# A gate projection whose squares, root and gated sums stand elsewhere, and another order of the second mixers' steps

## Chip, cores and metric

One core of a Trainium2 chip runs the whole program once. The metric is the device time of one execution in microseconds (us), the median of several; lower is better.

## What is computed

Two transformer blocks over 256 tokens of width 1024, in float32 accuracy. The change touches the seam between them: the gated addition that ends the first block, the two norms behind it, and the mixers of the second block.

```python
# end of the first block
g = jax.nn.sigmoid(rmsnorm(h, norm_ple_g) @ ple_gate)
h = h + g * (p @ ple_proj)
x = rmsnorm(h, final_norm_g)
# second block
proj = rmsnorm(x, mix_norm_g) @ w_in          # (256, 2328)
conv_a, conv_b, q, k_c, v_c, k_s, v_s, k_w, v_w, gate_logits = jnp.split(proj, IN_SPLITS, axis=-1)
y_conv = silu(layernorm(depthwise_conv31(conv_a * sigmoid(conv_b)), ...))
y_nsa = nsa_mixer(q, k_c, v_c, k_s, v_s, k_w, v_w, gate_logits, ...)   # three attentions, rotary on q, k_s, k_w
h = x + jnp.concatenate([y_conv, y_nsa], axis=-1) @ w_out
h = h + memory_attention(...)
h = h + peer(...)
```

## The kernel before, in words

Every dense product streams its weights from HBM in units of 128 x 1024 floats (four units a chunk, four buffers `raw`). ScalarE (ACT) rounds a unit's two halves into `w_hi` (`split_hi`, L421), VectorE (DVE) or GpSimd (POOL) subtracts the rest into `w_lo` (`split_lo`, L428), and TensorE (PE) makes three products with `x_hi` and `x_lo` (L494). There are two slots of `w_hi` and `w_lo`, so a unit's split can begin only when PE has used the unit two before it. `s_use1`, `s_use` count units used (first, second half), `s_hi1`, `s_hi`, `s_lo1`, `s_lo` the split halves, `s_ev` the chunks evacuated. All queues are in order: a wait holds back all that stands behind it on its engine.

**The gate projection** (`ple_and_norm`) has two chunks, one for each half of the 1024 columns. `split_chunks` emits, for ACT and for DVE, a body for the first chunk (not "hooked": units 2 and 3, then unit 0 of the next chunk, with the `lead` functions behind unit 2, 3 and `UNITS`), and a "hooked" body for the second (unit 1, hook 0, units 2 and 3, hook 1, unit 0 of what follows). On ACT the first body has the squares of `h` behind units 2 and 3 (`own_square`, L1870) and the square root behind unit 0 of the next chunk (`own_root`, L1875); DVE inverts it (`own_inverse`, L1879). In the second body, ACT's hook 0 waits for all products of the first chunk and makes the first half's gates, one sigmoid for each token tile (L1891); hook 1 squares `h` and `xn` (L1916). DVE's hook 0 (`gated_sum`) waits for `s_ev`, then makes for each of the two token tiles a product with `ple` (L1903), the sum into `h` (L1905) and the gained copy `xn` (L1907), all ahead of the split of unit 2. PE's last unit does token tile 0, then the transposes of the new `h` (L893), then tile 1.

Behind the two bodies stand the second half's gates (L1932), the `x_hi` and `x_lo` of the next projection (L902, L909), sums (L1937, L1939) and, last on DVE, the second half's gained copies (L1953, tokens `gained`).

**The second mixers** (`mixers_2`) are six strands of steps, each a Python generator: `d` dense (12 units of w_in in token-major form, 4 steps each, then 8 units in feature-major form, then w_out's 8 units), `c` conv taps on PE and the layer norm, `t` conv taps on DVE (11 taps of 4 tiles, L2126 and L2130), `k` keys and token tile 0 of the attention, `q` queries and token tile 1, `n` the norm. `weave` takes them in the order of the letters of `MIXERS_2_ORDER` and puts each step's instructions at the ends of the engines' queues; a step whose inputs aren't emitted yet gives nothing. When the letters are used up, the strands go on in turn. The dense strand's step that begins unit 1 has `other_half`: PE transposes the other half of `h` and ACT and DVE make its `x_hi` and `x_lo`. The steps of `n` are: squares of `h` and `xn` for tile 0 (L2000, L2002), the same for tile 1, a bias from them on DVE (L2006 to L2009), the roots (L2013), the inverse (L2016), then the inverse turned by PE (L2022). The first chunk's evacuation (L704) waits for the inverse. `c` begins with an identity and the diagonals of the first taps on POOL (L2082, L2078). The half of a unit that POOL splits is the first.

## Time and profile before

| | |
|---|---|
| median of 3 runs | 1627.99 us (1622.12 to 1630.15) |
| the profiled execution | 1626.81 us, its span 1624.8 us |
| mean granted clock of TensorE | 0.985 |
| PE | 1553.3 us busy (96%) |
| DVE | 1183.0 us (73%) |
| ACT | 858.5 us (53%) |
| POOL | 342.6 us (21%) |
| end of the gate projection's first chunk | about 497 us |
| second mixers, w_in | 511.8 to 594.1 us |
| second mixers, no dense products | 594.1 to 676 us |
| w_out | from 676 us |

PE is busy nearly all the time over the whole span, so the thing to read is where it is not, and where its granted clock is low: in those places something else sets the pace. A line of the timeline ends with the idle time of its engine before it and the instruction that ended it. In a table of stretches, each engine's busy time is followed by its number of instructions; PEclk is the granted clock as a share of 2.4 GHz.

### The profile page before, as it was taken

Reading aid. Unit: us, or ns where it says so; the run is one execution under the profiler, and the core shown is the slowest. Engines: PE = TensorE matmul, PEld = TensorE weight load, DVE = VectorE, ACT = ScalarE, POOL = GpSimd, SP = SyncE. Lnnn points to the kernel's source line nnn. Section 1 sums busy time; section 2 is a strip of 40 time slices with the busy share of each in tenths; the row PEclk is TensorE's granted clock in tenths of the full one; section 3 lists DMA queues with packets and bytes.
Section 4 is the critical chain, followed back from the end, with each engine's and each line's share of the span. In section 5 each row is a group of like instructions: output and inputs, shape, how many; then the busy total and the mean of one; then the engine's idle time right before and its main releaser. Section 6 shows DMA issues by size and latency. Waiting matters only on the chain.

```text
span 1624.8 us, 31457 instructions
## 1 busy us (share of the span) xinstructions
PE 1553.3 (96%) x10528; PEld 1409.2 (87%) x10528; DVE 1183.0 (73%) x2258; ACT 858.5 (53%) x1573; POOL 342.6 (21%) x257
## 2 busy tenths in 40 slices
PE   8899998999998888999999999999999999999997
PEld 8789987999876776898998999988888999999996
DVE  3788676788657558555489677779998777776776
ACT  5664445656557644566455455554444454445444
POOL 3334322011000501132057755530000000000000
PEclk9999999999999988999999999999999999999999
DMA  7333244555565610164546644467777665566554
GB/s 278 118 112 97 92 143 163 169 169 179 183 194 155 241 42 1 53 202 148 167 146 206 201 146 137 142 191 242 241 243 224 197 190 182 192 182 190 184 186 149
DMA packets 87847, 271.14 MB, mean 167 GB/s; under 512 B 9824, under 2 KB 26336, under 8 KB 87392
## 3 DMA queue, kind: packets, MB, share of 16 engines
q1 hardware_dynamic: 65088, 237.01, 45.8%
q10 hardware_dynamic: 22688, 33.17, 6.5%
q8 instruction: 47, 0.77, 0.2%
q14 instruction: 24, 0.20, 0.0%
HBM read 258.60 MB, written 11.53 MB: 166 GB/s over the span
## 4 chain that ended last, share of the span: by engine, by line
PE 81%; DVE 9%; ACT 4%; issue 3%; POOL 2%; DMA 1%; ACTq 1%; DVEq 0%; SPq 0%; POOLq 0%
PE ps_chunk L494 44%; PE ps_misc L494 21%; PE ps_misc L295 7%; PE ps_misc L2729 4%; PE ps_chunk L295 2%; ACT w_hi L421 1%; DVE ffn_arena L1743 1%; POOL w_lo L428 1%; DVE w_lo L428 1%; PE ps_misc L936 1%; PE ps_chunk L501 1%; DMA raw<-in_stream 0%; ACT ffn_arena L1727 0%; PE ps_chunk L936 0%; POOL mixers_arena L2078 0%
## 5 line engine op out<-in xcount | busy, mean ns | idle before, releaser
L421 ACT ACTIVATE w_hi<-raw 128x512 fp32r<-128x512 f32 (+1 forms) x900 | 548.7, 626 | 490.2 <-PE ps_chunk L494 284.4
L428 DVE TENSOR_TENSOR w_lo<-raw,w_hi 128x512 fp32r<-128x512 f32 x671 | 488.1, 743 | 270.7 <-ACT w_hi L421 260.8
L494 PE MATMUL ps_chunk<-x_hi,w_hi 128*128 128x256 f32 x1792 | 518.7, 289 | 14.4 <-POOL w_lo L428 7.3
L494 PE MATMUL ps_chunk<-x_hi,w_lo 128*128 128x256 f32 x1792 | 508.2, 284 | 0.0
L494 PE MATMUL ps_chunk<-x_lo,w_hi 128*128 128x256 f32 x1792 | 507.9, 283 | 0.0
L428 POOL TENSOR_TENSOR w_lo<-raw,w_hi 128x512 fp32r<-128x512 f32 (+2 forms) x229 | 298.9, 1319 | 542.8 <-ACT w_hi L421 479.6
L494 PEld LDWEIGHTS ps_chunk<-x_hi,w_hi 128*128 128x128 f32 x1792 | 344.3, 192 | 27.3 <-POOL w_lo L428 12.7
L494 PEld LDWEIGHTS ps_chunk<-x_hi,w_lo 128*128 128x128 f32 x1792 | 344.8, 192 | 2.8 <-issue 0.2
L494 PEld LDWEIGHTS ps_chunk<-x_lo,w_hi 128*128 128x128 f32 x1792 | 344.5, 192 | 0.0
L494 PE MATMUL ps_misc<-w_hi,hid_hi 128*128 128x512 f32 x520 | 203.5, 391 | 2.1 <-DVE hid_lo L2808 1.4
L494 PE MATMUL ps_misc<-w_hi,hid_lo 128*128 128x512 f32 x520 | 203.1, 391 | 0.0
L494 PE MATMUL ps_misc<-w_lo,hid_hi 128*128 128x512 f32 x520 | 202.3, 389 | 0.0
L295 PE MATMUL ps_misc<-mixers_arena 128*128 128x128 f32 (+7 forms) x840 | 116.3, 298 | 7.7 <-ACT mixers_arena L1393 2.8
L295 PEld LDWEIGHTS ps_misc<-mixers_arena 128*128 128x128 f32 (+1 forms) x840 | 105.6, 198 | 15.7 <-ACT mixers_arena L966 3.4
L494 PEld LDWEIGHTS ps_misc<-w_hi,hid_hi 128*128 128x128 f32 x520 | 97.9, 188 | 21.7 <-issue 1.6
L494 PEld LDWEIGHTS ps_misc<-w_lo,hid_hi 128*128 128x128 f32 x520 | 97.6, 188 | 20.9
L494 PEld LDWEIGHTS ps_misc<-w_hi,hid_lo 128*128 128x128 f32 x520 | 97.9, 188 | 17.6
L494 PE MATMUL ps_chunk<-w_hi,x_hi 128*128 128x512 f32 (+2 forms) x256 | 102.2, 399 | 5.6 <-DVE w_lo L428 3.2
L494 PE MATMUL ps_chunk<-w_hi,x_lo 128*128 128x512 f32 (+2 forms) x256 | 98.0, 383 | 0.0
L494 PE MATMUL ps_chunk<-w_lo,x_hi 128*128 128x512 f32 (+2 forms) x256 | 97.7, 382 | 0.0
L2804 DVE TENSOR_TENSOR xn<-row,peer_arena 128x256 f32<-128x256 f32 x128 | 80.7, 631 | 10.1 <-PE ps_misc L494 7.4
L2719 DVE TENSOR_TENSOR xn<-ident_iota,ps_chunk 128x512 f32<-128x512 f32 x64 | 43.8, 684 | 43.1 <-PE ps_misc L2729 39.5
(372 smaller groups left out, 1724.1 us busy)
## 6 DMA issues: line engine op xcount, KB each, us to landing
raw<-in_stream SPq DMA_DIRECT2D x452, 512.0 KB, 3.6
early_rows<-row ACTq DMA_DIRECT2D x64, 128.0 KB, 1.7
row<-early_rows ACTq DMA_DIRECT2D x62, 128.0 KB, 3.3
memory_kv<-mixers_arena ACTq DMA_DIRECT2D x4, 512.0 KB, 4.9
mixers_arena<-in_cmp_w ACTq DMA_DIRECT2D x1, 2048.0 KB, 10.3
mixers_arena<-memory_kv ACTq DMA_DIRECT2D x4, 512.0 KB, 6.8
mixers_arena<-in_consts ACTq DMA_DIRECT2D x1, 1729.0 KB, 9.0
row<-in_rows ACTq DMA_DIRECT2D x3, 512.0 KB, 7.3
```

Source lines behind the costliest of these rows:

```text
L295: return lambda e: e.matmul(out, lhsT, rhs, start=start, stop=stop, skip_group_check=True)
L421: e.activation(w_hi[q % 2][:, s], raw[q][:, s], ACT.Copy).then_inc(made, 1)
L428: e.tensor_tensor(w_lo[q % 2][:, s], raw[q][:, s], w_hi[q % 2][:, s].bitcast(F32), ALU.subtract).then_inc(made, 1)
L494: last = e.matmul(o, stationary[a], moving[b], start=start and i == 0, stop=stop and i == 2, skip_group_check=True)
L501: e.matmul(o, a[:, k * P:(k + 1) * P], x_hi[:, k, :], start=start and i == 0, stop=False, skip_group_check=True)
L936: done = pe.do(lambda e, i=i, s=s: e.transpose(ps[0:rows_out, i * P:(i + 1) * P], s, ident), *needs, *free)
L1743: e.scalar_tensor_tensor(out=o, in0=ps_chunk[slot][:, piece * T:(piece + 1) * T - lag], scalar=col[:, bass.ds(at + (2 - lag), 1)], in1=o, ...
L2719: e.tensor_tensor(cols_hot[g % 2], same, against(1), ALU.is_equal).then_inc(s_eq, 1)
L2729: last = e.matmul(ps_misc[:, g, i * P:(i + 1) * P], cols_hot[g % 2][:, i, :], rows_hot[g % 2][:, i, :], start=True, stop=True)
L2804: e.tensor_tensor(own[b], gel[slot], g, ALU.mult).then_inc(s_own, 1)
```

## The change

In the gate projection: ACT's first square goes ahead of unit 2, the second behind unit 2, the root behind unit 3, and a one-column sigmoid stands where the root stood, so the sigmoid's table is loaded there. DVE's inverse goes behind unit 3. `gated_sum` is split by token tile: tile 0 behind unit 1 and tile 1 behind unit 2 of the second chunk, each waiting for its own gate; the gained copies go behind unit 3, and the squares of the gained copies move to two new steps of `n` in the second mixers. The strings of the order differ throughout: 358 letters for 352, `n` 8 for 6, `d` 134 for 130, the others alike.

```diff
-MIXERS_2_ORDER = ("dddddddnndddnnndnkqddddqdddcdddddddddddqdddddddddddkqddddddckdkddddddddkcqdddddddddtdcqkkddqdtdddkdqdkcddkk"
-                  "kkkkkkcqddqdcdkqktddkdqqqkcddtqttttctktctkqttttdkcttttccttttddktttcqqkkkqqtdtttdqdtdkcttddktddctcqdd"
-                  "cctctdcdcttcckdqqtkktdkttdqqtdttcqddtttttttdcckkdttdttqqtckttqtccttdtdcdccdcccccdccddkddckddddkqktqq"
-                  "ccdcdtdtdqcccccccdkcddkqqdckkdqqkcqkqccckqqkc")
+MIXERS_2_ORDER = ("ndncddddnddddcnkddtnddddndnnqcdddddqdddddddtdddddkddddddddddqddkdkcdddqddddqddddkdddddddkkqkdddkqdkd"
+                  "qqdcdddkkkkdctkqkddddkddkktcqqqdddkkddcqqtdkdtktttttttdcttdkddtqddttddttktkktddccqqqttkcqddddddqkttt"
+                  "ttttcdcctdttcttktddkdqqkctttqcccccdttqtctttdkdttttttkkctttdtqtctkqqcdcddtckttcctqqttcccccccdcktcddcc"
+                  "kqkqqtcdcccckkdddddccccqqctkddcqccddkkkqccdddqkqkqdcqdkqcd")
...
                     def after(u):
-                        if not hooked and u in lead:
-                            lead[u](e)
+                        at = ("next", u) if hooked else u
+                        if at in lead:
+                            lead[at](e)
                     for q in range(begin, 2):
                         split(e, q, n)
                     hook(0)
+                    after(0)
                     for q in range(2, UNITS):
...
-            def gated_sum(e, slot, m):
-
-                if m != first:
-                    return
-                cols = halves[0]
-                e.wait_ge(s_ev, first + 1)
-                for t in range(TT):
+            def gated_sum(t):
+
+                def run(e):
+                    cols = halves[0]
+                    e.wait_ge(s_gate_0, t + 1)
                     e.tensor_tensor(gate[:, t, cols], gate[:, t, cols], ple[:, t, cols], ALU.mult).then_inc(s_ple, 1)
                     e.wait_ge(s_ple, t + 1)
                     e.tensor_tensor(h[:, t, cols], h[:, t, cols], gate[:, t, cols], ALU.add).then_inc(s_ple_sum[t], 1)
-                    e.wait_ge(s_ple_sum[t], 1)
-                    e.tensor_tensor(xn[:, t, cols], h[:, t, cols], row[:, cols], ALU.mult).then_inc(s_gain[t], 1)
...
+            def first_gains(e, slot, m):
 
                 if m == first:
                     cols = halves[0]
-                    for src, made, at, over in ((h, s_ple_sum, PART, gate), (xn, s_gain, 10, ple)):
-                        for t in range(TT):
-                            e.wait_ge(made[t], 1)
-                            e.activation(over[:, t, cols], src[:, t, cols], ACT.Square,
-                                         accum_out=ss[:, at + t:at + t + 1]).then_inc(s_square, 1)
+                    for t in range(TT):
+                        e.wait_ge(s_ple_sum[t], 1)
+                        e.tensor_tensor(xn[:, t, cols], h[:, t, cols], row[:, cols], ALU.mult).then_inc(s_gain, 1)
+
+            def first_squares(e, slot, m):
+
+                if m == first:
+                    cols = halves[0]
+                    for t in range(TT):
+                        e.wait_ge(s_ple_sum[t], 1)
+                        e.activation(gate[:, t, cols], h[:, t, cols], ACT.Square,
+                                     accum_out=ss[:, PART + t:PART + t + 1]).then_inc(s_square, 1)
+
+            def sigmoids_table(e):
+                e.activation(ss[:, 24:25], c("one"), ACT.Sigmoid)
...
-            split_chunks(first, count, act_hooks=(hook, first_squares), dve_hooks=(gated_sum,), ahead=1,
-                         act_lead={2: own_square(0), 3: own_square(1), UNITS: own_root}, dve_lead={UNITS: own_inverse})
+            act.quiet(own_square(0))
+            split_chunks(first, count, act_hooks=(hook, first_squares), dve_hooks=(None, first_gains), ahead=1,
+                         act_lead={2: own_square(1), 3: own_root, UNITS: sigmoids_table},
+                         dve_lead={3: own_inverse, ("next", 0): gated_sum(0), ("next", 2): gated_sum(1)})
...
-                    both = act.do(lambda e, t=t: e.activation(scratch, xn[:, t, half], ACT.Square,
-                                                              accum_out=ss[:, 2 + t:3 + t]), gained[t])
+                    act.do(lambda e, t=t: e.activation(scratch, xn[:, t, half], ACT.Square,
+                                                       accum_out=ss[:, 2 + t:3 + t]), gained[t])
                     yield
-                dve.wait((s_square, 2 * TT))
+                for t in range(TT):
+                    both = act.do(lambda e, t=t: e.activation(scratch, xn[:, t, 0:CW], ACT.Square,
+                                                              accum_out=ss[:, 10 + t:11 + t]), first_gained)
+                    yield
+                dve.wait((s_square, TT))
```

## Rows read from the trace of the kernel before

**Rows 1.** Stretches: length, busy us of each engine, granted clock, DMA share, GB/s

```profile
511.80:551.30 39.50, 33.07 (x163) 26.77 (x163) 24.81 (x52) 25.52 (x53) 14.89 (x13) 0.96 0.68 236
...
551.30:594.10 42.80, 38.97 (x289) 37.82 (x288) 17.93 (x31) 21.49 (x35) 13.41 (x10) 0.88 0.34 109
...
594.10:676.00 81.90, 70.44 (x642) 54.77 (x639) 66.50 (x139) 37.93 (x103) 6.48 (x3) 0.87 0.01 1
```

**Rows 2.** Timeline, gate projection; start, us, engine, line, operation, [idle before <-releaser]

```profile
500.52 0.69 DVE L1903 TENSOR_TENSOR ffn_arena<-ffn_arena 128x512 f32<-128x512 f32 x1 [1.92 <-ACTq L1894]
...
505.37 0.50 PE L494 MATMUL ps_chunk<-w_hi,x_hi 128*128 128x512 f32 x1 [2.74 <-DVE w_lo L428]
...
511.39 0.39 PE L494 MATMUL ps_chunk<-w_hi,x_lo 128*128 128x512 f32 x1
...
511.61 0.39 PE L494 MATMUL ps_chunk<-w_lo,x_hi 128*128 128x512 f32 x1
```

**Rows 3.** Timeline of ACT, the first half's gates

```profile
497.88 1.28 ACT L1891 ACT_TABLE_LOAD   x1
...
499.18 1.26 ACT L1891 ACTIVATE ffn_arena<-ps_chunk,ss 128x512 f32<-128x512 f32 x2
```

**Rows 4.** Timeline, start of the second mixers, ACT, DVE, POOL and PE

```profile
515.73 1.57 ACT L902 ACTIVATE x_hi<-ps_misc,ss 128x256 fp32r<-128x256 f32 x4 [1.59 <-PE ps_misc L878]
...
516.17 1.28 DVE L1953 TENSOR_TENSOR xn<-h,row 128x512 f32<-128x512 f32 x2
...
517.17 1.17 ACT L421 ACTIVATE w_hi<-raw 128x512 fp32r<-128x512 f32 x2
...
517.96 1.28 POOL L428 TENSOR_TENSOR w_lo<-raw,w_hi 128x512 fp32r<-128x512 f32 x1 [91.62 <-ACT w_hi L421]
...
518.21 0.64 ACT L2000 ACTIVATE picks<-h 128x512 f32<-128x512 f32 x1
...
519.30 0.50 PE L494 MATMUL ps_chunk<-w_hi,x_hi 128*128 128x512 f32 x1 [0.65 <-POOL w_lo L428]
...
521.14 0.19 ACT L2002 ACTIVATION_READ_ACCUMULATOR picks<-xn 128x1 f32 x1
...
525.39 0.48 PE L2022 MATMUL ps_misc<-ident_iota,picks 128*128 128x128 f32 x1 [3.75 <-DVE picks L2019]
```

**Rows 5.** Timeline of POOL and PE, the diagonals of the conv taps

```profile
548.55 0.32 POOL L2082 TENSOR_TENSOR mixers_arena<-ident_iota 128x64 f32<-128x64 f32 x1
...
548.95 5.17 POOL L2078 TENSOR_TENSOR mixers_arena<-mixers_arena,col 128x1280 f32<-128x1280 f32 x2
...
555.43 0.38 PE L494 MATMUL ps_chunk<-x_hi,w_hi 128*128 128x256 f32 x1 [1.08 <-POOL w_lo L428]
```

**Rows 6.** Timeline of DVE and POOL, a pair that overlaps later

```profile
631.41 2.67 POOL L2078 TENSOR_TENSOR mixers_arena<-mixers_arena,col 128x1280 f32<-128x1280 f32 x1 [13.99 <-PE ps_chunk L295]
...
631.97 2.13 DVE L1010 TENSOR_TENSOR mixers_arena<-mixers_arena 128x4 f32<-128x4 f32 x1
```

**Rows 7.** Timeline of PE and DVE, rotary embedding and last dense product

```profile
567.01 0.41 PE L936 MATMUL ps_misc<-ident_iota,mixers_arena 128*64 128x128 f32 x2 [1.52 <-DVE mixers_arena L2226]
...
592.01 0.30 PE L936 MATMUL ps_misc<-ident_iota,mixers_arena 128*64 128x128 f32 x1 [1.23 <-DVE mixers_arena L2226]
...
592.56 0.63 PE L295 MATMUL ps_misc<-mixers_arena 128*64 128x30 f32 x6
...
594.14 0.69 DVE L708 TENSOR_TENSOR mixers_arena<-ps_chunk,picks 128x512 f32<-128x512 f32 x1 [1.87 <-PE ps_chunk L494]
```

**Rows 8.** Busy times by stretch, two stretches at a low clock

```profile
524.90:528.40 3.50, 3.01 (x8) 2.48 (x9) 2.40 (x7) 0.87 (x2) 0.79 (x1) 0.51 1.06 296
...
579.60:589.80 10.20, 10.20 (x51) 10.09 (x51) 1.49 (x2) 3.81 (x7) 1.28 (x1) 0.50 0.15 51
```

**Rows 9.** DVE in the stretch without dense products: busy times, then who waited

```profile
594.00:665.50 71.50, 60.04 (x547) 44.37 (x545) 62.86 (x133) 33.26 (x93) 5.04 (x2) 0.86 0.01 1
...
DVE mixers_arena L979 <- PE ps_misc L295: 5.1, 7, 2.5
```

More of the change, by code:

```diff
@@ L1905, in gated_sum @@
                     e.tensor_tensor(h[:, t, cols], h[:, t, cols], gate[:, t, cols], ALU.add).then_inc(s_ple_sum[t], 1)
-                    e.wait_ge(s_ple_sum[t], 1)
-                    e.tensor_tensor(xn[:, t, cols], h[:, t, cols], row[:, cols], ALU.mult).then_inc(s_gain[t], 1)
+                return run
+            def first_gains(e, slot, m):
[4 more added lines that the diff above has]
+                        e.tensor_tensor(xn[:, t, cols], h[:, t, cols], row[:, cols], ALU.mult).then_inc(s_gain, 1)
             def first_squares(e, slot, m):
@@ L1912, in first_squares @@
                     cols = halves[0]
-                    for src, made, at, over in ((h, s_ple_sum, PART, gate), (xn, s_gain, 10, ple)):
-                        for t in range(TT):
-                            e.wait_ge(made[t], 1)
-                            e.activation(over[:, t, cols], src[:, t, cols], ACT.Square,
-                                         accum_out=ss[:, at + t:at + t + 1]).then_inc(s_square, 1)
+                    for t in range(TT):
[4 more added lines that the diff above has]
+                e.activation(ss[:, 24:25], c("one"), ACT.Sigmoid)
             s_gate_0 = sem("s_gate_0")
             s_ple, s_square = sem("s_ple"), sem("s_square")
-            s_gain = [sem(f"s_gain{t}") for t in range(TT)]
+            s_gain = sem("s_gain")
             dve.wait(have_gain)
             act.wait(*added[1])
-            split_chunks(first, count, act_hooks=(hook, first_squares), dve_hooks=(gated_sum,), ahead=1,
-                         act_lead={2: own_square(0), 3: own_square(1), UNITS: own_root}, dve_lead={UNITS: own_inverse})
+            act.quiet(own_square(0))
+            split_chunks(first, count, act_hooks=(hook, first_squares), dve_hooks=(None, first_gains), ahead=1,
+                         act_lead={2: own_square(1), 3: own_root, UNITS: sigmoids_table},
+                         dve_lead={3: own_inverse, ("next", 0): gated_sum(0), ("next", 2): gated_sum(1)})
             second = first + 1
@@ L1954, in ple_and_norm @@
                              sum_made[t], own=False) for t in range(TT)]
-            return next_x, both_gains, sum_made, gained, s_square
+            return next_x, both_gains, sum_made, gained, s_square, (s_gain, TT)
         def own_norm(*turned):
@@ L1966, in own_norm @@
             return act.do(lambda e: e.activation(h[:, 1, :], xn[:, 1, :], ACT.Copy, scale=ss[:, 17:18]), inverse)
-        next_x, both_gains, sum_made, gained, s_square = ple_and_norm(added)
+        next_x, both_gains, sum_made, gained, s_square, first_gained = ple_and_norm(added)
         def mixers_2():
@@ L2001, in norm @@
                            sum_made[t])
-                    both = act.do(lambda e, t=t: e.activation(scratch, xn[:, t, half], ACT.Square,
-                                                              accum_out=ss[:, 2 + t:3 + t]), gained[t])
+                    act.do(lambda e, t=t: e.activation(scratch, xn[:, t, half], ACT.Square,
+                                                       accum_out=ss[:, 2 + t:3 + t]), gained[t])
                     yield
-                dve.wait((s_square, 2 * TT))
+                for t in range(TT):
[3 more added lines that the diff above has]
+                dve.wait((s_square, TT))
                 dve.do(lambda e: e.tensor_scalar(bias, ss[:, PART:PART + TT], EPS / D, EPS * EPS, ALU.mult, ALU.add))
                 dve.do(lambda e: e.scalar_tensor_tensor(out=bias, in0=ss[:, 10:12], scalar=1.0 / D, in1=bias,
-                                                        op0=ALU.mult, op1=ALU.add))
+                                                        op0=ALU.mult, op1=ALU.add), both)
                 v = dve.do(lambda e: e.scalar_tensor_tensor(out=bias, in0=ss[:, 16:18], scalar=EPS / D, in1=bias,
-                                                            op0=ALU.mult, op1=ALU.add), both)
+                                                            op0=ALU.mult, op1=ALU.add))
                 yield
```

## Prediction

> **What bounds the kernel now.** I read the page's busy times first (PE 96% of the span), then the busy times of five stretches around the change, then the waits of PE in each, and last the timeline of each engine at those waits. PE sets the pace, so only its idle time and its stretches at a low clock can be won. From the first unit of w_in to the last product before w_out they are large [rows 1]: 6.4 us of 39.5 idle, then 3.8 of 42.8, then 11.5 of 81.9, with mean granted clocks of 0.96, 0.88 and 0.87 of 2.4 GHz. In the first two PE waits for single late instructions. In the third DVE is the fuller engine: 62.9 of 71.5 us busy, where 5.1 us of its idle time waits for PE's scores [rows 9]. So there the length is that of DVE's queue, and an order can win only DVE's few gaps. Earlier, in the gate projection, PE stands still for 2.74 us until DVE has split unit 2 [rows 2].
>
> **The change part by part.** The sum is made on the profiled execution, 1626.8 us, which is 1.2 below the median of 1628.0.
>
> *1. Gate projection: -2.7 us.* DVE makes six operations of 0.69 us from 500.52, then the split, and PE goes on at 505.37 [rows 2]. After the change only two of the six stand ahead of the split. They also start sooner: the sigmoid's table (1.28 us, at 497.88) is loaded before the products end, and DVE waits for one gate, not for both (1.26 us the pair) [rows 3]. I put the start near 499, the two operations until 500.4, ACT's rounding of unit 2, which stands behind the gates, at 499.6 to 500.3, and so the split's first half at about 501.1. PE asks for it at 502.6. The cover is 1.5 us; unit 3 has two more operations ahead of its split, and some 1.3 us of cover. Squares and root come 1.2 to 2.5 us sooner on ACT, ahead of unit 2's rounding; PE has two units (12 products of 0.22 to 0.23 us each, 2.7 us [rows 2]) before it asks for that one. Moved squares cost ACT as much as before. Next late in this place: nothing within 0.5 us. The whole stall goes.
>
> *2. Start of the second mixers: +0.7 us, between -1.5 and +4.2.* I work in the clock of the old trace; all of it slides by part 1. The new order begins `n`, `d`, `n`: four squares now stand on ACT ahead of the step that holds `other_half`. Two of them wait for the gained copies, which are DVE's last work, 516.17 plus 1.28 us [rows 4]. So ACT, in order, is held: the first gained square can start at 516.9, and three more follow at 0.8 (four took from 518.21 to 521.33), until 519.3. Only then come the other half's `x_hi` (1.57, which had begun at 515.73), the rounding of unit 2 (0.6 for its first half) and POOL's part (1.28): PE can begin unit 2 at 522.8, not at 519.30. PE ended unit 1 at 518.65, so its idle time here grows from 0.65 to 4.15 us. Against that, the turned inverse now stands behind 16 dense steps instead of 11, and PE's 3.75 us idle before L2022 [rows 4] has five steps (3.4 us) to hide behind. But the `c` step with the diagonals is now emitted inside unit 2, so 0.32 + 5.17 us of POOL [rows 5] lie between its parts of units 3 and 4: unit 3's ends at about 524.8, the diagonals at 530.3, unit 4's (0.8, it is narrow) at 531.1. PE, two units and the turn later, would be there at 528.9. In the old trace it reached unit 4 at about 530.5, so we lose some 0.6. Behind it the first chunk's evacuation and the rounding of unit 5 keep this distance; own_norm now stands behind unit 6's rounding, a small gain I leave out. The low clock after the old wait, 3.5 us at 0.51 [rows 8], has a counterpart after the new one, which the wait for POOL covers. Bounds: -1.5 if POOL's diagonals stop nobody, +4.2 if the new idle time comes on top of the old.
>
> DVE's small operations meet the diagonals as well. Once, in the old trace, a 128x4 product with two inputs beside POOL's 2.67 us multiplication took 2.13 us and ended with it [rows 6]. Here the bias, unit 4's second half and the wide copy of the inverse would wait in that manner, until 530.6, and the turn until 531.6; with that, unit 4 starts at 531.9 and not at 531.1, and I use 0.7 as the middle. The Trainium skill (SBUF — State Buffer, Who interferes with whom) has this as a rule that speaks against the change: a VectorE instruction with two SBUF inputs and a GpSimd one that reads SBUF exclude each other for their whole length. Without the rule the loss would be 0.6, by it 1.4; the pair of rows agrees with it.
>
> *3. Diagonals gone from their old place: -1.1 us.* There they stood ahead of POOL's part of a split, and PE waited 1.08 [rows 5]. Between 0 and -1.1.
>
> *4. Rotary embedding of the keys: -1.5 us.* PE waited 1.52 for it [rows 7]; its DVE step was emitted behind the evacuation of unit 15's chunk and unit 16's first product. The new order emits it ahead of both, directly behind unit 15's last step, while PE still has most of that unit (2.9 us) to do. Between 0 and -1.5.
>
> *5. End of the dense products: -2.4 us.* The queries' rotation stood ahead of the last dense steps and held PE for 1.23; six dense steps now lie between the rotation and its first turn, where two did. Four turns (0.55 to the next start) and six small products (0.56) stood ahead of the last dense step and now stand behind it [rows 7]. DVE is idle for 1.87 at that moment, waiting for that last product, so DVE's queue starts sooner by all of it. Between -0.5 and -2.4.
>
> *6. Clock: 0, between 0 and -3.8 us.* PE is at half clock for 10.2 us from 579.6 [rows 8], 3.2 us into a run of 56 small products of 30 columns (the compression's). The new order cuts this run to 32, then lays dense steps between. If the clock stays up, 17 dense products of 0.21 us shrink to 0.12 and 30 small ones of 0.20 to 0.12: 1.6 + 2.2. No row says at which length it falls, and 32 still last about 3.9 us, so I take 0.
>
> *7. The stretch without dense products: 0, between -4 and +5.* It has the same 43 taps, softmaxes and norm on DVE (one of the 44 taps lies earlier in both orders). It begins sooner by what parts 1 to 5 bring, and since DVE's queue sets its length it ends sooner by as much. Bounds: DVE's waits for PE of 5.1 us [rows 9] nearly gone, or doubled.
>
> Sum: -2.7 + 0.7 - 1.1 - 1.5 - 2.4 = -7.0, 1619.8 us on the profiled execution, 1621.0 on the median's scale. I say 1620.5, a little for the open side of part 6. After w_out nothing is changed and PE is full, so nothing is given back there.
>
> **The rivals.** *More than that:* the clock stays up in the compression (-3.8) and DVE's gaps in the last stretch shrink by half (-2.5): 1614. For it: the order is wholly new in that stretch, and its 0.86 mean clock [rows 9] leaves room. Against: DVE's work there is fixed. *The gains are absorbed:* parts 3 to 5 shift waits only, because the last stretch's DVE queue waits for PE elsewhere, or part 2 comes out at +4; the gate's 2.7 remains: 1625.5. To it belongs that the gate's stall doesn't go, because another wait (a split's ACT half) takes its place. *Slower:* in the last stretch the new order puts score products and the DVE step that reads them side by side at six of the eight large softmaxes, where the old did so at three, and the last exponentials of both tiles follow one another with little of DVE's work between. Where DVE isn't behind PE at such a place, it waits for the products, as once for 2.47 us (half of the 5.1 in rows 9). Six such waits and one exponential (2 us) are some 17 us, 12 more than now: 1633. It decides as soon as DVE's idle time in this stretch grows by more than 7 us.
>
> **How the numbers follow.** Forecast (1616 to 1625): 0.45. More: 0.23. Absorbed: 0.20. Slower: 0.12. The unknown costs reach from about -15 to +9 in all; to leave out no more than two in ten I take 1612 to 1631. Half a per cent is 8.1 us, about what a measurement of this kernel can tell from none (its three runs lie 8 apart). Below 1619.9 lie the second case and some 0.17 of the first: 0.40. Above 1636.1 lies part of the last and what I have not seen: 0.08. The rest, 0.52, is within it.
>
> **What would show it.** Right: no wait of PE between the first chunk's end and the turn in the gate projection; one wait of about 4 us before unit 2 of the second mixers; the wait before L2022 gone or under 1 us; the diagonals at about 520 to 528; no wait of PE for L2226; the last dense product 6 to 9 us sooner; DVE over 85% busy from there to the layer norm. Wrong: a wait for a split in the gate projection; a second long wait at unit 4; DVE under 80% busy in the last stretch, or waiting for PE over 10 us; the low clock again at length while dense products run.

## The result, and the profile after

The changed kernel takes 1632.99 us in the median (1626.08 to 1639.35, 14 runs), the kernel before beside it 1627.12 (1621.84 to 1630.15, 14 runs): ratio 1.0040 [1.0024, 1.0056]. The medians lie 5.9 us apart, where 7 us less were forecast, and the time is outside the range. Both profiled executions begin the gate projection within 0.05 us of each other (485.75 and 485.80), so their times can be set side by side.

| | before | after | difference |
|---|---|---|---|
| profiled execution (span) | 1626.81 (1624.8) | 1637.04 (1634.9) | +10.2 |
| mean granted clock | 0.985 | 0.975 | |
| first product of the second mixers | 511.8 | 508.8 | -3.0 |
| last dense product of w_in | 593.8 | 589.0 | -4.8 |
| first value product of the attention | 660.38 | 655.56 | -4.8 |
| first product of w_out | 675.96 | 684.33 | +8.4 |

The changed kernel is ahead until the value products begin and behind when they end. Of the 1.8 us that come on top behind w_out's first product, 1.0 are its first products, which still run at half clock. The stretches, as [rows 1, 8, 9] had them (length, busy us of PE, PE's weight loads, DVE, ACT, POOL with their counts, then the granted clock, the DMA share and GB/s):

```profile
506.60:546.40 39.80, 34.12 (x172) 27.88 (x171) 26.06 (x43) 27.65 (x59) 13.85 (x13) 0.96 0.67 236
546.40:589.20 42.80, 39.96 (x284) 39.35 (x282) 24.66 (x44) 20.99 (x34) 14.35 (x10) 0.84 0.35 108
589.20:684.60 95.40, 82.79 (x652) 67.49 (x652) 66.45 (x138) 38.18 (x106) 6.19 (x3) 0.76 0.03 10
...
588.90:660.40 71.50, 58.89 (x542) 43.46 (x540) 62.31 (x132) 33.72 (x96) 4.74 (x2) 0.85 0.02 7
```

The third stretch is 13.5 us longer than in [rows 1], PE is 12.4 us busier in it, and its clock is 0.76 instead of 0.87; DVE does the same work (66.45 and 66.50 us). So the time didn't go into a wait: PE does the same products more slowly. PE's timeline of the changed kernel shows which:

```profile
647.18 0.66 PE L938 MATMUL ps_chunk<-ident_iota,mixers_arena 128*128 128x128 f32 x4
...
651.03 1.11 PE L938 MATMUL ps_misc<-ident_iota,mixers_arena 128*128 128x128 f32 x4 [3.19 <-DVE mixers_arena L1013]
651.93 1.06 PE L938 MATMUL ps_chunk<-ident_iota,mixers_arena 128*128 128x128 f32 x4
653.80 1.97 PE L938 MATMUL ps_misc<-ident_iota,mixers_arena 128*128 128x128 f32 x8 [0.81 <-DVE mixers_arena L1013]
...
655.56 13.75 PE L295 MATMUL ps_misc<-mixers_arena 128*128 128x64 f32 x64
669.11 1.92 PE L938 MATMUL ps_chunk<-ident_iota,xn 128*128 128x128 f32 x8
670.81 13.75 PE L295 MATMUL ps_misc<-mixers_arena 128*128 128x64 f32 x64
```

and that of before the same place, which the prediction didn't look at:

```profile
655.74 1.97 PE L936 MATMUL ps_chunk<-ident_iota,mixers_arena 128*128 128x128 f32 x8 [3.68 <-DVE mixers_arena L2112]
657.50 3.08 PE L936 MATMUL ps_misc<-ident_iota,mixers_arena 128*128 128x128 f32 x12
...
660.38 7.80 PE L295 MATMUL ps_misc<-mixers_arena 128*128 128x64 f32 x64
668.01 1.04 PE L936 MATMUL ps_chunk<-ident_iota,xn 128*128 128x128 f32 x8
668.89 7.26 PE L295 MATMUL ps_misc<-mixers_arena 128*128 128x64 f32 x64
```

These are the 128 value products (probabilities by values, 64 columns each). With the eight transposes between they last 15.8 us in before and 29.0 in after: 13.2 us, all at one place. The busy times over just that stretch, after:

```profile
655.60:684.60 29.00, 29.00 (x138) 29.00 (x138) 8.47 (x11) 8.13 (x14) 1.45 (x1) 0.50 0.07 19
```

and before:

```profile
660.40:676.20 15.80, 15.80 (x138) 15.80 (x138) 8.43 (x12) 8.13 (x14) 1.44 (x1) 0.96 0.00 1
```

PE is busy without a gap in both; the granted clock is 0.50 (1.2 GHz) in one and 0.96 in the other. In the records the low clock lasts from 654.7 to 661.5 us in before and from 649.0 to 686.6 in after. It falls in a wait in both, the 3.68 and the 3.19 us one. In before it is back 1.1 us into the value products and stays; in after it doesn't come back while they run, only 2.2 us after w_out's wide products have begun. The Trainium skill (TensorE: Matmul & The Clock Gate, HAM oscillation) tells of such falls in waits, and these two rows agree. They also show the clock staying low while PE is busy for 29.00 of 29.00 us.

### The profile page after: what moved, and what is told of

It is laid out like the page before. It is cut to its first block, busy times and chain, and to the rows that moved or that the text cites. A ratio compares the mean times of both kernels' runs of the same rounds, so it can differ in the third digit from the quotient of the medians.

```text
span 1634.9 us, 31462 instructions
## 1 busy us (share of the span) xinstructions
PE 1566.6 (96%) x10528; PEld 1424.1 (87%) x10528; DVE 1189.1 (73%) x2258; ACT 857.5 (52%) x1574; POOL 342.3 (21%) x257
## 4 chain that ended last, share of the span: by engine, by line
PE 80%; DVE 9%; ACT 4%; issue 3%; DMA 1%; POOL 1%; ACTq 1%; DVEq 0%; SPq 0%; POOLq 0%
PE ps_chunk L496 43%; PE ps_misc L496 21%; PE ps_misc L295 8%; PE ps_misc L2744 3%; PE ps_chunk L295 2%; POOL w_lo L428 1%; ACT w_hi L421 1%; DVE ffn_arena L1745 1%; DVE w_lo L428 1%; DMA raw<-in_stream 1%; PE ps_misc L938 1%; PE ps_chunk L503 1%; DVE mixers_arena L2145 0%; ACT ffn_arena L1729 0%; PE ps_chunk L938 0%
## 5 line engine op out<-in xcount | busy, mean ns | idle before, releaser
L496 PEld LDWEIGHTS ps_chunk<-x_hi,w_hi 128*128 128x128 f32 x1792 | 345.5, 193 | 29.9 <-POOL w_lo L428 12.4
L295 PE MATMUL ps_misc<-mixers_arena 128*128 128x128 f32 (+7 forms) x840 | 128.4, 319 | 7.7 <-ACT mixers_arena L968 3.2
L295 PEld LDWEIGHTS ps_misc<-mixers_arena 128*128 128x128 f32 (+1 forms) x840 | 117.5, 217 | 15.6 <-issue 3.8
## 6 DMA issues: line engine op xcount, KB each, us to landing
mixers_arena<-in_cmp_w ACTq DMA_DIRECT2D x1, 2048.0 KB, 10.2
```

What stands on the lines that cost most here:

```text
L295: return lambda e: e.matmul(out, lhsT, rhs, start=start, stop=stop, skip_group_check=True)
L496: last = e.matmul(o, stationary[a], moving[b], start=start and i == 0, stop=stop and i == 2, skip_group_check=True)
```

## Experiments

Each profile, of one execution, gives the length of the 128 value products, with the transposes between them. Each ratio, with its 95% interval in brackets, is to executions of the kernel before that ran beside that experiment, so it isn't the median over one fixed number.

| kernel | median (range, runs) | ratio to before | value products |
|---|---|---|---|
| changed kernel | 1632.99 (1626.08 to 1639.35, 14) | 1.0040 [1.0024, 1.0056] | 29.0 us |
| gate_only | 1622.49 (1618.47 to 1626.31, 10) | 0.9962 [0.9934, 0.9990] | 15.7 |
| order_only | 1635.51 (1631.02 to 1642.76, 10) | 1.0045 [1.0009, 1.0080] | 22.9 |
| warm_av | 1629.72 (1622.23 to 1637.68, 10) | 1.0014 [0.9992, 1.0036] | 15.2 |
| warm_gap | 1626.68 (1617.97 to 1630.60, 10) | 1.0005 [0.9983, 1.0028] | 15.2 |
| tail_old | 1621.79 (1618.71 to 1625.37, 10) | 0.9952 [0.9922, 0.9981] | 15.2 |
| diag_late | 1634.99 (1629.45 to 1638.97, 10) | 1.0039 [1.0014, 1.0065] | 23.0 |
| squares_late | 1629.87 (1623.99 to 1637.82, 10) | 1.0016 [0.9994, 1.0038] | 29.0 |
| warm_before | 1629.85 (1625.53 to 1633.88, 10) | 1.0009 [0.9993, 1.0026] | 15.2 |
| one_letter | 1626.46 (1620.12 to 1628.35, 10) | 0.9987 [0.9957, 1.0016] | 15.2 |
| tail_new | 1636.57 (1632.43 to 1641.85, 10) | 1.0055 [1.0023, 1.0086] | 29.0 |
| three_moves | 1619.17 (1616.66 to 1623.18, 12) | 0.9959 [0.9938, 0.9980] | 15.2 |
| fill_gap | 1624.62 (1619.38 to 1629.16, 10) | 0.9983 [0.9967, 0.9999] | 15.2 |

### Which half of the change costs

`gate_only` has the changed gate projection with the old order, in which two more `n` stand behind the first two, for the two new steps. `order_only` has the old gate projection with the new order.

```diff
-MIXERS_2_ORDER = ("dddddddnndddnnndnkqddddqdddcddddd"
+MIXERS_2_ORDER = ("dddddddnnnnddddnnndnkqddddqdddcddddd"
...
```

> The gate projection's change alone: the old order, with only two letters n put behind the first two for the two squares that moved (1.6 us of ScalarE). Theory one (the order brought TensorE's half clock onto the attention's value products, and that is the loss): 2.7 us won in the gate projection, up to 1.6 given back ahead of the turned inverse, the value products at the clock of the kernel before (16 us for 128 rows), so 0.997 to 1.000 of the time before. Theory two (the gate's change itself costs, by its squares in the second mixers): 1.003 or more, with the last dense product of w_in no sooner than 593.8 us.

> The new order alone, on the gate projection of before. Theory one: as in the changed kernel the value products fall into a stretch at 1.2 GHz (29 us instead of 16), and the gate's 2.7 us are missing, so 1.004 to 1.007. Theory two (the gate's change costs): 0.996 to 1.000.

The gate projection alone makes the kernel faster, 0.9962; the order alone makes it slower, 1.0045, as much as the whole change. `gate_only` reaches its first unit of the second mixers 3.1 us sooner. It then pays back 2.1 of them (1.5 by a longer wait: 5.28 us idle ahead of the turned inverse, where before had 3.75 [rows 4], since two more squares stand in front of the roots), and has them again at the last dense product (3.8 us sooner). `order_only` is 5.2 us ahead of before at the last dense product and 5.6 behind at w_out; its clock is low for 20.5 us, over the first 64 value products and the beginning of the others (13.75 us for 64, then 7.65).

### Products to keep PE at work

`warm_av` adds 16 products whose results nobody reads ahead of the value products; `warm_gap` adds 12 in PE's idle time behind the first transposes of the layer norm, and 8 ahead of the value products. `warm_before` is the kernel before with those 20.

```diff
+                if t == 0:
+                    pe.wait(*free)
+                    for _ in range(16):      # 8 in warm_gap and warm_before
+                        pe.quiet(mm(ps, x_hi[:, 0, 0:P], x_hi[:, 0:2, :].rearrange("p k t -> p (k t)")))
                 for hd in range(NSA_H):
```

> The changed kernel with 16 further products of 512 columns in front of the attention's value products, into the bank that these then overwrite (their results are used by nobody). Theory one: 16 products cost 3.7 us at full and 7 us at half clock; they bring the clock to 2.4 GHz, the 128 rows of value products take 16 us instead of 29, so 6 to 9 us less than the changed kernel: 0.998 to 1.000 of before. Rival (the clock is not what costs, or busy products here do not raise it): 4 to 7 us more than the changed kernel, 1.006 or more.

> The changed kernel with 12 such products in TensorE's idle gap of 3.2 us before the last softmaxes and 8 in front of the value products. Theory one: the 12 cost nothing (2.8 us in a gap of 3.2) and keep the clock from falling, the 8 cost 1.9 us at full clock, so 9 to 12 us less than the changed kernel: 0.996 to 0.999 of before, and no stretch at half clock from 649 to 686 us. Rival: 2 to 5 us more than the changed kernel.

> The kernel before, with 20 added products of 128 columns by 256, whose results nobody reads: 12 in PE's idle time behind the first turn of the layer norm, 8 ahead of the value products (the same two places in which they brought the changed kernel 6 us). Theory (clock): before already runs its value products at full clock in most of its executions, so the added products bring 0 to 2 us: median 1625 to 1627, ratio 0.998 to 1.001. Rival (the products help anything): they bring as much here as in the changed kernel, 4 to 6 us, and then their gain there says nothing of what the new order lost. Rival (they cost): each product of 0.11 us lies on the path, 20 of them 2 us: 1628 to 1629.

With added work PE keeps or regains the clock, and the changed kernel gets 4 to 6 us back (by the ratios) although it has more to do. Both come out some 2 us dearer than expected (1.0014 and 1.0005, where at most 1.000 and 0.999 were), which their intervals don't exclude as noise. In `warm_gap` the 12 products (3.02 us) fill most of the wait, and no low clock is recorded there at all. In the kernel before the same 20 products bring nothing (1.0009), so what they heal is something that the changed kernel has and the kernel before, in most of its executions, has not. (An added product is 128x512 in the rows, about 0.25 us at full clock and 0.5 at half; the expectation of `warm_before` took it to be 0.11.)

### The last letters of the order

`tail_old` is the changed kernel with the last 54 letters of the old order. The lines are the ends of the two orders. `tail_new` is the kernel before with the last 57 letters of the new order. In both one `t` (a tap on DVE) ahead of these letters is left out or put in, so that their number stays 67.

```diff
-kqkqqtcdcccckkdddddccccqqctkddcqccddkkkqccdddqkqkqdcqdkqcd
+kdddkqktqqccdcdtdtdqcccccccdkcddkqqdckkdqqkcqkqccckqqkc
```

> The changed kernel, with the last 54 letters of its order (from the seventh mask softmax to the layer norm's second step) taken from the order of before; everything up to some 640 us stands as in the changed kernel. Theory (clock): what PE does in the last 10 us ahead of the value products sets the clock in which they run. In before it is 3.7 us of idle time in one piece, then transposes and products close together, and PE is at full clock again within 1 us of the first value product; in the changed kernel it is 3.2 us, then a few products, then 0.8 us more, and the 128 products take 29.0 us instead of 15.8. With the old tail the profile should show the value products at full clock (16 to 18 us), w_out's first product 8 to 12 us sooner than in the changed kernel, and a median of 1621 to 1627. Rival (queue): the new order's loss comes from DVE's and ACT's order in the whole stretch from 590 us on, and the clock only follows; then the last letters alone bring less than 2 us and the value products still take over 25 us. Rival (phase): the outcome depends on the instant at which the stretch falls, not on its order; then the run to run spread stays as wide as the changed kernel's (1626 to 1639) with the median between the two.

> The kernel before (its gate projection, its order), with only the last 57 letters of its order taken from the changed kernel's. Theory (clock): this is the new order's whole loss, carried into the old kernel: the value products run at half clock (25 to 29 us instead of 15.8) in most executions, w_out's first product comes 9 to 13 us later, median 1634 to 1640, ratio 1.005 to 1.008. Rival (queue): the loss is spread over the stretch from 590 us on, then under 3 us come with these letters (1626 to 1630). Rival (phase): the instant matters and not the order; the old kernel comes to this place some 5 us later than the changed one, and the clock then may stay full: 1626 to 1630 with a wide spread.

It works in both directions. The old tail takes the changed kernel from 1.0040 to 0.9952; the new tail takes the kernel before from 1 to 1.0055. No engine's work differs, only its order. The stretch of the value products in `tail_new`:

```profile
658.50:687.50 29.00, 29.00 (x138) 29.00 (x138) 8.49 (x11) 8.13 (x14) 1.45 (x1) 0.50 0.07 19
```

and in `tail_old`:

```profile
654.10:669.40 15.30, 15.30 (x139) 15.30 (x138) 8.81 (x12) 8.49 (x15) 1.44 (x1) 1.00 0.00 1
```

In `tail_new` the clock had fallen before the long wait (2.73 us here), at 645.9 us, in a run of 16 products behind a wait of 1.72:

```profile
645.24 4.93 PE L295 MATMUL ps_misc<-mixers_arena 64*128 64x128 f32 x16
```

The same 16 last 3.00 us in before.

Is it the instant that decides, and not the order? Not alone: `tail_new` and `tail_old` come to their value products at 658.5 and 654.1 us (655.6 in after, 660.4 in before), and each has the clock that its last letters give it. The mean clocks of all executions say the same: with the new tail (after, `order_only`, `diag_late`, `squares_late`, `tail_new`) it is 0.978 or less in 29 of 54, with the old tail or one of the two repairs below (`gate_only`, `tail_old`, `three_moves`, `one_letter`, `fill_gap`) in none of 52. But the instant has a part. In after and `squares_late` the clock falls 2 us before the long wait ends and stays low for 37.5 us; in `order_only` and `diag_late`, with the same last letters, it falls within 0.4 us behind the wait's end and stays low for 20.5. And the kernel before pays at times too: in 9 of 103 executions it took 1638.6 to 1643.9 us at a mean clock of 0.973 to 0.977, in all others 1633.2 or less. That the value products were slow in those nine is likely by the size of the step, but none of them was profiled. So the order sets how often this is paid, not whether in each execution.

### What in the last letters

In the new tail four transposes of the layer norm (tile 0) stand ahead of PE's long wait, which leaves it 3.19 us long, and a wait of 0.81 lies behind it, between two groups of eight. In the old tail all of the layer norm's transposes are behind the long wait, and PE has 20 products without a gap before the value products. `one_letter` moves one `c`, those four transposes, ten letters back:

```diff
-kqkqqtcdcccckkdddddccccqqctkddcqccddkkkqccdddqkqkqdcqdkqcd
+kqkqqtcdcccckkdddddccccqqctkddcqccddkkkqcdddqkqkqdccqdkqcd
```

> The changed kernel, with one letter of its order moved: the layer norm's turn of tile 0 (four products of PE) ten letters later, directly ahead of that of tile 1. In the changed kernel PE does these four before a 3.19 us wait, then runs 8 products, waits 0.80 us, runs 8 more and begins the value products, all at half clock to 686.6 us. With the letter moved the long wait begins some 0.65 us sooner (3.8 us, as in before), and 12 products or more follow it close together. No work, no wait of DVE and no length of anything else is changed. Theory (clock): if how PE's work lies in these few us sets the clock of the value products, this letter alone may bring it back: value products 16 to 18 us instead of 29.0, w_out's first product 8 to 12 us sooner, median 1622 to 1628. Rival (more is needed): the 0.80 us wait that stays, or the smaller amount of work, is enough to leave the clock low; then nothing changes (1631 to 1635), and the cause lies in the rest of the last letters.

One letter takes the ratio from 1.0040 to 0.9987. Its timeline of PE has the 20 products in one piece, and the value products at full clock:

```profile
656.15 1.12 PE L938 MATMUL ps_misc<-ident_iota,mixers_arena 128*128 128x128 f32 x4 [3.78 <-DVE mixers_arena L1013]
657.06 1.92 PE L938 MATMUL ps_chunk<-ident_iota,mixers_arena 128*128 128x128 f32 x8
658.93 1.57 PE L938 MATMUL ps_misc<-ident_iota,mixers_arena 128*128 128x128 f32 x8
...
660.33 7.26 PE L295 MATMUL ps_misc<-mixers_arena 128*128 128x64 f32 x64
```

But the letter changes two things, the length of the long wait and the gap behind it. `fill_gap` leaves the long wait and puts four unread products into the gap:

```diff
                                  copy_evac(act, PT[:, (t + 1) * b + k, g * 512:(g + 1) * 512]))
+                        if (t, b, g) == (0, 1, 1):
+                            busy_pe(4)
```

> The changed kernel with 4 added products of 128 columns by 256, whose results nobody reads, directly behind the transposes of tile 0's last softmax: they fall into the 0.80 us in which PE waits for tile 1's last multiplication, and last some 0.9 us at half clock. The 3.19 us wait ahead of them stays as it is. Theory (the short gap): PE must be at work without a break behind the long wait for its clock to rise before the value products begin; then these 4 products alone bring it back in most executions: value products 15 to 18 us instead of 29.0, median 1622 to 1628. Rival (place of the long wait): it is where and how long PE waits ahead of this (3.19 us here, 3.7 to 3.8 in the kernels that kept the clock) that counts; then the value products stay at 25 to 29 us and the median at 1631 to 1635.

```profile
655.41 0.89 PE L946 MATMUL ps_misc<-ident_iota,mixers_arena 128*128 128x128 f32 x4 [3.19 <-DVE mixers_arena L1021]
655.95 2.06 PE L295 MATMUL ps_misc<-x_hi 128*128 128x512 f32 x4
657.81 1.05 PE L946 MATMUL ps_chunk<-ident_iota,mixers_arena 128*128 128x128 f32 x4
658.65 1.26 PE L946 MATMUL ps_misc<-ident_iota,mixers_arena 128*128 128x128 f32 x8
659.75 2.46 PE L295 MATMUL ps_misc<-mixers_arena 128*128 128x64 f32 x21
```

The wait of 3.19 us is still there, the gap of 0.81 is not, and the clock is back at 659.1 us, 0.6 ahead of the value products, which take 15.2 us. So what PE does between the long wait and the value products is enough to decide it, with the long wait as it was. The profiled execution alone wouldn't show it, since its clock fell only at 655.7 us, just behind the wait's end, and not 2 us before it as in after; but none of the ten executions is over 1629.16 us or under a clock of 0.981, where 11 of the changed kernel's 14 take longer than 1631. The four products (2.06 us) do more than fill 0.81 us, though: whether it is the gap's absence or their added work that counts, these runs don't tell apart.

### The two early waits of the new order

`squares_late` puts the first two steps of `n` back behind seven dense steps; `diag_late` issues POOL's diagonals 37 letters later. The lines are the starts of the orders of the changed kernel and `squares_late`.

```diff
-ndncddddnddddcnkddtn
+dddddddnncnddcnkddtn
```

> The changed kernel, with the first 16 letters of its order rearranged (the same letters): the two square steps of the norm stand behind the first seven dense steps, as in before, not ahead of the first. Theory (held ACT): PE's 3.99 us of idle time ahead of unit 2 is ACT's queue, held by the squares that wait for DVE's gained copies; it falls to 0.6 to 1 us, and unit 2 comes 3.0 to 3.4 us sooner. Whether that stays: if it does, the last dense product is 3 us sooner too (median 1629 to 1631 with the clock over the value products as in the changed kernel). Rival (inverse): the turned inverse then is the next late thing, since its squares end no sooner, and PE waits 2 to 4 us ahead of its product (L2022) or for the first chunk's evacuation; the last dense product is then less than 1 us sooner and the early wait of the new order costs nothing by itself.

> The changed kernel, with one conv step of its order moved: the first of the two that stand ahead of the diagonals goes 37 letters later, so that POOL's 0.32 and 4.89 us multiplications are issued behind unit 18 rather than beside the keys' and queries' rotation angles. Theory (port): in the changed kernel DVE's small two-input operations beside these multiplications take 2.2 us each instead of 0.17, the split behind them is late, and PE waits 2.84 us for it. Without the neighbour these operations take under 0.5 us, this wait of PE goes (0 to 0.5 us), and the last dense product comes 2.5 to 3 us sooner than in the changed kernel; the median, with the clock over the value products unchanged, 1629 to 1632. Rival (queue): the split is late because of the amount of work that the rotation angles put ahead of it on DVE, whoever stands beside it; then the wait shrinks by less than 1.5 us. Rival (moved): the diagonals now stand ahead of POOL's part of a split near unit 18 and PE waits there for as long as it did before (1.1 us or more).

In `squares_late` unit 2 is at once 3.4 us sooner (0.65 us idle instead of 3.99), but waits of 1.74 and 2.05 us for POOL's part of a split follow at units 3 and 5, and by the end of the token-major units 0.6 are left. That is the size that the rival forecast, though not its wait: PE stands only 0.36 us ahead of the turned inverse. Behind it the wait at the diagonals is longer than the changed kernel's 2.84 us, and the last dense product is 2.0 us later than there:

```profile
552.24 0.58 PE L496 MATMUL ps_chunk<-x_hi,w_hi 128*128 128x256 f32 x1 [4.26 <-DVE w_lo L428]
```

In `diag_late` the 2.84 us stall is gone, no idle time over 0.5 us is left between 539 and 592 us, and no wait takes its place; a small DVE operation that took 2.23 us takes 0.17:

```profile
548.35 0.17 DVE L2254 TENSOR_SCALAR mixers_arena<-mixers_arena 128x16 f32<-128x16 f32 x1
```

Yet the last dense product is only 0.55 us sooner than in after, where 2.5 to 3 were expected. In this execution, as in that of `tail_old`, whose first 66 letters are the same, ACT had to wait for the weights of unit 8, by 2.6 and 2.2 us. The row of `tail_old`:

```profile
535.49 1.15 ACT L421 ACTIVATE w_hi<-raw 128x512 fp32r<-128x512 f32 x2 [2.19 <-DMA raw<-in_stream]
```

That wait is 1.3 us in after and 1.6 in two pieces in before. What sets its length isn't shown. It isn't being ahead of time alone: `gate_only`, 1 to 2 us ahead of before there, has no such wait, `three_moves`, some 4 ahead, one of 0.6 us, and `order_only`, behind it, one of 1.8. `diag_late`'s median (1634.99) is no better than the changed kernel's, and it keeps the new tail, and the low clock with it.

### All three moves

> The changed kernel with the three moves of its order tried one by one, together: squares behind the first seven dense steps, diagonals 37 letters later, the last letters from before. Each of PE's three early waits (3.99, 2.84 and the low clock over the value products) is taken away. Theory (the weights' stream is next): ahead of unit 8 or 9 ACT's rounding waits 1.1 to 3.0 us for the stream of weights in most of the profiled executions with the new head, and this takes back what the first two moves bring; so the result is that of the old tail alone, 1619 to 1623, ratio 0.993 to 0.997. Rival (they add): without the diagonals' stall the early gain is kept, the last dense product comes 7 to 9 us sooner than in before, 1615 to 1619, ratio 0.991 to 0.993. Rival (DVE takes it back): the stretch without dense products begins sooner but ends when it did, because its queue is DVE's and longer; then the last dense product is early and the value products are not.

`three_moves` has the squares late, the diagonals late and the old tail. Its median of 1619.17 us is the shortest of all kernels here; its ratio, 0.9959 [0.9938, 0.9980], can't be told from that of `tail_old` or of `gate_only`. In its profiled execution the weights came in time (0.6 us of waiting), the last dense product is 10.3 us sooner than in before and w_out 11.5. So the early moves can pay; that they do so in the median isn't shown.

## Why the prediction was wrong

- **Part 1, gate projection, -2.7 us: right, -3.0.** Unit 2's split no longer has six operations ahead of it but two, and DVE begins the first at 498.55, not 500.52 [rows 2]. PE has no wait in the projection; the second mixers begin 3.0 us sooner, and `gate_only` shows that the time is kept.

```profile
498.55 0.69 DVE L1903 TENSOR_TENSOR ffn_arena<-ffn_arena 128x512 f32<-128x512 f32 x1
499.27 0.69 DVE L1905 TENSOR_TENSOR h<-h,ffn_arena 128x512 f32<-128x512 f32 x1
499.90 1.45 DVE L428 TENSOR_TENSOR w_lo<-raw,w_hi 128x512 fp32r<-128x512 f32 x2
```

- **Part 2, +0.7: the wait was right, the sum 1.4 us too dear.** The idle time before unit 2 came out at 3.99 us (4.15 forecast), for the reason given: ACT was held by the squares.

```profile
519.63 0.80 PE L496 MATMUL ps_chunk<-w_hi,x_hi 128*128 128x512 f32 x1 [3.99 <-POOL w_lo L428]
```

  The wait ahead of the turned inverse is gone (3.75 in [rows 4]). The diagonals, however, were not issued inside unit 2: their step waits for the first chunk's evacuation to be emitted, so that the `c` there gave nothing. By the end of the token-major units after is 3.7 us ahead, which makes part 2 -0.7. (The forecast's 0.7 isn't the middle of its own 0.6 and 1.4 either; that is 1.0.)

- **Part 3, -1.1: wrong, it was +3.3.** The diagonals came two `c` later, behind unit 11's split, and there met what part 2 feared for another place. POOL in the changed kernel:

```profile
545.27 4.89 POOL L2093 TENSOR_TENSOR mixers_arena<-mixers_arena,col 128x1280 f32<-128x1280 f32 x2
```

  DVE beside it, and the same operation when POOL is elsewhere:

```profile
545.47 2.23 DVE L2254 TENSOR_SCALAR mixers_arena<-mixers_arena 128x16 f32<-128x16 f32 x1
...
547.95 2.24 DVE L2257 SCALAR_TENSOR_TENSOR mixers_arena<-mixers_arena 128x16 f32<-128x16 f32 x1
...
552.06 1.63 DVE L428 TENSOR_TENSOR w_lo<-raw,w_hi 128x512 fp32r<-128x512 f32 x1
...
554.03 0.17 DVE L2254 TENSOR_SCALAR mixers_arena<-mixers_arena 128x16 f32<-128x16 f32 x1
```

  The operations end with POOL's two multiplications, at 547.7 and 550.2; the split behind them is late and PE waits:

```profile
552.06 0.39 PE L496 MATMUL ps_chunk<-x_hi,w_hi 128*128 128x256 f32 x1 [2.84 <-DVE w_lo L428]
```

  In before it was 1.08 [rows 5]. The 3.7 us of lead are 0.5 at the third feature-major unit. The Trainium skill (SBUF — State Buffer, Who interferes with whom) has one of the two engines stand still until the other is done, and names VectorE's `tensor_scalar` among the operations that can take the shared ports. The first row, with one input, agrees (2.23 us against 0.17), and `diag_late` shows that the stretching goes with its neighbour.

- **Parts 4 and 5, -3.9 together: right, -4.3.** The keys' rotary wait (1.52 [rows 7]) is gone, though nothing of it shows at the sixth feature-major unit (0.6 us ahead), because PE's turns for the attention stand earlier; at the eighth unit it is 2.3, at the last dense product 4.8.

- **Part 6, clock, 0: right where it looked.** The long low stretch of the compression is there as before, 10.2 us at 0.50 from 577.4 us [rows 8].

- **Part 7, 0 between -4 and +5: right up to the value products, and it stopped there.** From the last dense product to the first value product both kernels need 66.6 us; DVE is busy for 62.31 of 71.50 (62.86 in [rows 9]), and its waits for PE's scores are shorter, not longer. So the rival "slower" had the sign, but its mechanism, DVE's waits, didn't happen (5.1 us of waiting for scores in [rows 9], 2.6 here), and that its 1633 us meets the measured median is luck:

```profile
DVE mixers_arena L981 <- PE ps_misc L295: 2.6, 4, 1.8
DVE mixers_arena L710 <- PE ps_chunk L496: 2.2, 1, 2.2
```

- **The step that failed** is part 7's: "since DVE's queue sets its length it ends sooner by as much". That holds up to the first value product. The last 15.8 us of the stretch are PE's, busy for 15.80 of 15.80 us, and most of them lie behind the window that part 7 read, which ends at 665.5 us [rows 9]. They stood in [rows 1], inside a mean clock of 0.87, and were taken as fixed, because part 6 weighed the clock only where the order cuts a run of small products. In its place the runs showed a term of +13.2 us in the profiled execution: the value products take 15 us at the full clock, 29 at the low one and 23 where it rises half way, and which of these is paid depends on a few products ahead of them, whose order the change rewrote. A bound was to be had: 15.8 us that are bound by PE last up to 31.6 at half clock. A term of 0 to +15.8 us in the sum would have put the measured time inside the range.

The bounds as the parts give them add up to -17.0 and +6.0 us (+8.7 if the gate's stall stays), not to -15 and +9; nothing hangs on it.

The medians differ by less than the profiled executions do (5.9 and 10.2 us): the clock isn't the same in each execution. The changed kernel's 14 lie between 1626.08 us, at a mean clock of 0.983, and 1639.35 at 0.974. Nor does it vary only over the value products: `one_letter`, with the same order up to there, has it low for 13.7 us from 619.0 us, after for 3.4 from 618.3. Multiplying the share of the clock not granted by the span gives about what it costs in each (too much, where PE was waiting): 35.1 us in the mean for the changed kernel, 26.2 for before (the 31 executions of the first set), 23.5 for `tail_old`, 35.5 for `tail_new`. The rest of the time, by the same working, is 1598.1, 1601.4, 1598.4 and 1601.6: without the clock, the change is worth 3.3 us, about what its first part was to bring, and the new order nearly nothing (`order_only` 1601.2). That is an estimate from mean clocks, not a measurement.

## What to carry to other kernels

When the order of work is rewritten, read the granted clock not only where PE waits but over every long run of small products behind a wait, and put both levels of its length into the range. A wait can cost more than its length: here one of 3.19 us was followed by products that took 13.2 us longer, and moving four transposes to the far side of it was worth 6.5 us between the medians. Since the clock differs between executions of one kernel, its effect is judged by many executions, not by one profile. An emission order must be followed through each step's own conditions: a letter that gives nothing moves its work to a later one.

## What the runs showed of the hardware

- Of 64-column products, 64 took 13.75 us (0.215 each) at a granted clock of 0.50 and 7.26 (0.113) at 1.00. In the profiled executions of after, `squares_late` and `tail_new` the low clock outlasted all 128 of them, 29.0 us without a gap; in those of `order_only` and `diag_late` the first 64. In before and `gate_only` it rose some 1 us after the first of them. In the 14 profiled executions it never fell while they ran.
- It fell inside PE's long wait (3.19 to 3.78 us) in eight of these executions, within 0.4 us behind its end in four, in `tail_new` 1.7 us behind a wait of 1.72, and in `warm_gap`, whose longest wait there is 1.68 us, not at all.
- Small operations of VectorE (128x16), also one with one input from SBUF, lasted until GpSimd's large one ended: 2.23 us instead of 0.17.
- Six kernels with the same instructions up to unit 8 of the second mixers (after, `warm_av`, `warm_gap`, `tail_old`, `one_letter`, `fill_gap`) had ACT waiting for the weights of w_in by 1.3 to 3.0 us in all. One profiled execution of each can't settle a difference of 2 us in what lies behind.
